# Pre-norm's second half summed by GpSimd, an unscaled first tile, and two tiles closed by halves

## The reference

```python
h = rmsnorm(x, norm_pre[l, n])                    # x * rsqrt(mean(x * x) + eps) * gain
x = x + weight * rmsnorm(sublayer(h), norm_post[l, n])
```

## Time and profile before

| | |
|---|---|
| runs | 2857.49, 2858.16, 2862.65 us, median 2858.16 |
| profiled execution | 2856.87 us, span of its instructions 2854.0 us |
| TensorE's mean granted clock | .991 of full speed |
| VectorE, ScalarE, GpSimd busy | 52%, 37%, 4% of the span |
| products for the sums of x's squares (line 411) | 128, two records each |
| GpSimd's adds (line 1842) | 48 |

### The profile page before, as it was taken

One profiled execution on the slowest core, in us unless ns is written; L12 is line 12 of the kernel. 1 busy time (PEld: TensorE's weight loads), 2 busy tenths in 40 slices (PEclk: granted clock), 3 DMA queues, 4 the chain that ended last, 5 costly groups with the idle time before them and its releaser, 6 DMA issues.

```text
span 2854.0 us, 44258 instructions
## 1 busy us (share of the span) xinstructions
PE 2783.2 (98%) x18986; PEld 2587.9 (91%) x18986; DVE 1487.0 (52%) x2035; ACT 1064.2 (37%) x1559; POOL 106.8 (4%) x124
## 2 busy tenths in 40 slices
PE   8999999998999999999999999999989999999997
PEld 7999999997988889999999999999869988999996
DVE  5555326747564465552365553366576436555423
ACT  4333324325453343332243332242264434333322
POOL 0000000001100100000000000000001001000000
PEclk9999999999999999999999999999999999999998
DMA  4222322222233222232222322222223232222321
GB/s 113 81 81 84 93 82 62 70 73 78 88 105 102 62 67 81 86 88 82 76 74 81 88 86 83 77 73 60 76 78 111 82 95 62 81 86 83 88 84 62
DMA packets 420893, 232.95 MB, mean 82 GB/s; under 512 B 7124, under 2 KB 415736, under 8 KB 420760
## 3 DMA queue, kind: packets, MB, share of 16 engines
q1 hardware_dynamic: 414544, 210.33, 25.5%
q0 software_dynamic: 5984, 20.59, 2.2%
q10 hardware_dynamic: 232, 0.08, 0.0%
HBM read 219.44 MB, written 11.54 MB: 81 GB/s over the span
## 4 chain that ended last, share of the span: by engine, by line
PE 89%; DVE 6%; ACT 3%; DMA 1%; issue 1%; ACTq 0%; POOL 0%; DVEq 0%; POOLq 0%
PE PS L391 36%; PE PS L379 20%; PE PS L393 18%; PE PS L366 4%; PE PS L353 2%; PE PS L830 1%; DVE y_two L1387 1%; PE PS L549 1%; DVE x L1396 1%; PE PS L857 1%; DVE w_lo L1339 1%; DVE h_two L1347 1%; ACT w_hi L929 1%; DMA raw<-in_w_out_dram 1%; PE PS L645 1%
## 5 line engine op out<-in xcount | busy, mean ns | idle before, releaser
L391 PE MATMUL PS<-h_two,w_hi 128*128 128x288 f32 (+2 forms) x4032 | 922.9, 337 | 3.0 <-DVE gt L1418 3.0
L1339 DVE TENSOR_TENSOR w_lo<-raw,w_hi 128x1024 fp32r<-128x1024 f32 (+1 forms) x372 | 490.1, 1317 | 667.1 <-ACT w_hi L929 663.3
L929 ACT ACTIVATE w_hi<-raw 128x1024 fp32r<-128x1024 f32 (+1 forms) x372 | 413.6, 1112 | 592.6 <-DMA raw<-in_ffn_down_dram 268.4
L391 PEld LDWEIGHTS PS<-h_two,w_hi 128*128 128x128 f32 x4032 | 605.5, 188 | 3.7 <-issue 3.7
L393 PE MATMUL PS<-h_two,w_lo 128*128 128x288 f32 x2688 | 571.7, 294 | 0.0
L393 PEld LDWEIGHTS PS<-h_two,w_lo 128*128 128x128 f32 x2688 | 471.8, 188 | 58.3
L391 PE MATMUL PS<-a_two,w_hi 128*128 128x288 f32 (+2 forms) x1848 | 422.8, 337 | 0.0
L379 PE MATMUL PS<-h_two,w_hi 128*128 128x288 f32 x2048 | 381.3, 300 | 2.8 <-DVE proj L1648 1.9
L379 PEld LDWEIGHTS PS<-h_two,w_hi 128*128 128x128 f32 x2048 | 304.7, 189 | 8.1 <-issue 3.6
L391 PEld LDWEIGHTS PS<-a_two,w_hi 128*128 128x128 f32 x1848 | 277.5, 188 | 0.0
L393 PE MATMUL PS<-a_two,w_lo 128*128 128x288 f32 x1232 | 262.0, 294 | 0.0
(11 more groups left out here) (319 smaller groups left out, 3440.9 us busy)
## 6 DMA issues: line engine op xcount, KB each, us to landing
raw<-in_ffn_gu_dram SPq DMA_DIRECT2D x176, 512.0 KB, 3.9
raw<-in_ffn_down_dram SPq DMA_DIRECT2D x64, 704.0 KB, 4.6
raw<-in_w_in_dram SPq DMA_DIRECT2D x52, 512.0 KB, 3.8
raw<-in_w_out_dram SPq DMA_DIRECT2D x16, 512.0 KB, 4.1
raw<-in_w_mk_dram SPq DMA_DIRECT2D x16, 512.0 KB, 3.9
raw<-in_w_mv_dram SPq DMA_DIRECT2D x16, 512.0 KB, 4.0
raw<-in_w_mq_dram SPq DMA_DIRECT2D x16, 512.0 KB, 3.9
raw<-in_w_mo_dram SPq DMA_DIRECT2D x16, 512.0 KB, 4.0
```

The costliest lines, as they stand in the source:

```text
L391: mm(PW[slot][:, j, 0:c1 - c0], wt(ws)(0, k), row[:, c0:c1], start=begin, stop=end and j == 2, skip_group_check=True)
L929: A(whi(c % NW, slice(0, words)), rawu(c % NW, slice(0, words)), ACT.Copy).then_inc(whi_r, 1)
L1339: TT(wlo(c % NW, w_), rawu(c % NW, w_), f32(whi(c % NW, w_)), ALU.subtract).then_inc(wlo_r, 1)
```

## The change

- `pre_piece`, from pn = 1 on and for the second half: the eight squares go to a buffer of eight (`sqh`, two homes in SBUF) instead of the ring of four.
- `add_squares(pn)` on GpSimd, after its adds of the tiles' squares: it waits for the last of the eight squares of norm pn + 1 and adds them up in three instructions (four onto four pieces, two onto two, one onto one).
- TensorE: `opening` has no sums in its second half; one product, `pre_sum_second`, comes ahead of the k-step 1 of the third unit (FFN, IN), or ahead of k-step 4 of the first query unit of MVQ. In MK the sums of the first half stand beside units 1 to 4 and those of the second half are gone.
- The first unit's tile of F1, IN and F2 leaves PSUM by a copy on ScalarE (`raw_tile`), and VectorE scales the copy later.
- MO: `close_two` computes tiles 6 and 7 by halves (6 first half, 7 first half, 6 second half, 7 second half), with the squares, gains and GpSimd's add of tile 6 by halves too.
- The first six of the FFN's wide units are taken out of the loop; the sum of the second post half comes at k-step 1 in every opening.

```diff
@@ GpSimd
             def add_squares(pn):
-                for m in range(1, KD - 1):
-                    pool.wait_ge(psq_r, (KD - 1) * pn + m + 1)
+                whole = KD - 2 if pn % 4 == 2 else KD - 1
+                for m in range(1, whole):
+                    pool.wait_ge(psq_r, squares_before(pn) + m + 1)
...
+                if whole < KD - 1:
+                    pool.wait_ge(acc_r, added_before(pn) + whole - 1)
+                    for h in range(2):
+                        pool.wait_ge(psq_r, squares_before(pn) + whole + 1 + h)
+                        nc.gpsimd.tensor_tensor(acc[:, HALF[h]], acc[:, HALF[h]], sq[:, 0, HALF[h]], ALU.add).then_inc(acc_r, 1)
+                if pn == 4 * DEPTH - 1:
+                    return
+                to = second_home(pn + 1)
+                pool.wait_ge(qsq_r, upto(pn + 1, 1, KD - 1))
+                for n in (4, 2):
+                    nc.gpsimd.tensor_tensor(to[:, 0:n, :], to[:, 0:n, :], to[:, n:2 * n, :], ALU.add).then_inc(pstep, 1)
+                    pool.wait_ge(pstep, 2 * pn + (1 if n == 4 else 2))
+                nc.gpsimd.tensor_tensor(to[:, 0, :], to[:, 0, :], to[:, 1, :], ALU.add).then_inc(qadd_r, 1)
@@ TensorE
+            def pre_sum_second(pn):
+                pe.wait_ge(qadd_r, pn)
+                mm(PX[0][:, 1, 0:HT], ones, second_home(pn)[:, 0, :], start=True, stop=True).then_inc(qsq_d, 1)
+            def close_two(pn, a, t, hi, lo):
+                for h in range(2):
+                    for s in range(2):
+                        u = a + KD - 2 + s
...
+                        for k in range(KD):
+                            m = pieces(u % NW, s, h, k, hi, lo, 0, k == 0, k == KD - 1)
+                            if h == 1 and s == 0 and k == 0:
+                                post_begin(pn, 0)
+                                post_sum(pn, 0)
+                        m.then_inc(unit_d if h else (six_d, half_d)[s], 1)
@@ opening
-                        if h == 0 and k == sum_at:
+                        if h == 0 and k == 1:
+                            if (pn - 1) % 4 == 2:
+                                post_begin(pn - 1, 1)
                             post_sum(pn - 1, 1)
-                        pre_sum(pn, h, k)
+                        if h == 0:
+                            pre_sum(pn, h, k)
@@ ffn (TensorE)
+                for n in range(6):
+                    pe.wait_ge(tile_e, t + 1 + n)
+                    wide_unit(a + 2 + n, n % 2, (a + 2 + n) % NW, h_two, middle={1: lambda: pre_sum_second(pn)} if pn and n == 0 else None)
@@ MK and MVQ (TensorE)
-                    for j in (2 * m, 2 * m + 1):
-                        pre_sum(pn + 1, j // KD, j % KD)
+                    if 1 <= m <= KD // 2:
+                        for k in (2 * m - 2, 2 * m - 1):
+                            pre_sum(pn + 1, 0, k)
...
+                    if m == 0:
+                        beside[4] = lambda: pre_sum_second(pn)
@@ ScalarE
+                if pn and h:
+                    A(second_home(pn)[:, k, :], x[:, k, HALF[h]], ACT.Square).then_inc(qsq_r, 1)
+                    return
...
+            def raw_tile(to, a, slot):
+                act.wait_ge(unit_d, a + 1)
+                A(halves(to), PL[slot][:, :, 0:HT], ACT.Copy).then_inc(tile_e, 1)
...
+                    16: lambda: (raw_tile(proj[:, IN_PLACE[0], :] if pu == "F1" else sg, e, 0), pre_root(pn + 1, 1))})
@@ ffn (VectorE)
-                        v.wait_ge(unit_d, a + 1)
-                        TT(halves(gt[:, :]), PL[0][:, :, 0:HT], halves(rinv[:, :]), ALU.mult).then_inc(tile_e, 1)
+                        v.wait_ge(tile_e, t + 1)
+                        TT(gt[:, :], sg[:, :], rinv[:, :], ALU.mult).then_inc(gt_r, 1)
@@ MO (VectorE)
                 e = a + KD
+                seventh_y(pn, 0)
+                upcoming(e)
                 v.wait_ge(half_d, pn + 1)
                 last_y(pn, 0)
                 post_root(pn, 0)
-                last_y(pn, 1)
-                update(pn, 1.0, {5: lambda: upcoming(e + 1), 7: lambda: post_root(pn, 1)})
+                seventh_y(pn, 1)
+                update(pn, 1.0, {2: lambda: last_y(pn, 1), 5: lambda: upcoming(e + 1), 7: lambda: post_root(pn, 1)})
```

More of the change, by code:

```diff
@@ L109 @@
 WIDE = [(0, HT), (HT, HT + 512), (HT + 512, 2 * T)]
+pairs_before = lambda pn: sum(n % 4 == 2 for n in range(pn))
+squares_before = lambda pn: (KD - 1) * pn + pairs_before(pn)
+added_before = lambda pn: (KD - 2) * pn + pairs_before(pn)
 def hybrid_trunk(nc, i, o):
@@ L166, in hybrid_trunk @@
         mvT = place("mvT", [P, 4, NMEM], F32, G + 23552)
+        sqh = [place(f"sqh{n}", [P, KD, HT], F32, G + w_) for n, w_ in enumerate((19456, 4608))]
         xtok = place("xtok", [P, NCH + 1, D], F32, G)
@@ L382, in unit, with wide_unit @@
                 m.then_inc(unit_d, 1)
-            def wide_unit(u, slot, ws, two, kt=KD, k0=0, first=True, last=True):
+            def wide_unit(u, slot, ws, two, kt=KD, k0=0, first=True, last=True, middle=None):
                 pe.wait_ge(wlo_r, u + 1)
                 for k in range(kt):
+                    if middle and k in middle:
+                        middle[k]()
                     row = two[:, k0 + k, :, :].rearrange("p a t -> p (a t)")
@@ L394, in wide_unit, with post_begin @@
                 m.then_inc(unit_d, 1)
[L396 to L400, removed]
+            def post_begin(pn, h):
+                pe.wait_ge(acc_r, added_before(pn + 1) - (1 if pn % 4 == 2 and h == 0 else 0))
+                mm(PX[1][:, h, 0:HT], ones, acc[:, HALF[h]], start=True, stop=False, skip_group_check=True)
             def post_sum(pn, h):
@@ L469, in ffn @@
                 a, t = unit_base(l, pu), tile_base(l, pu)
-                opening(pn, a, t, sum_at=None if f % 2 else 1)
-                with pe.Fori(0, (2 * KF - 2) // 6) as r:
+                opening(pn, a, t)
+                for n in range(6):
+                    pe.wait_ge(tile_e, t + 1 + n)
+                    wide_unit(a + 2 + n, n % 2, (a + 2 + n) % NW, h_two, middle={1: lambda: pre_sum_second(pn)} if pn and n == 0 else None)
+                with pe.Fori(0, (2 * KF - 2) // 6 - 1) as r:
                     for n in range(6):
-                        pe.wait_ge(tile_e, r * 6 + (t + 1 + n))
-                        wide_unit(r * 6 + (a + 2 + n), n % 2, (a + 2 + n) % NW, h_two)
+                        pe.wait_ge(tile_e, r * 6 + (t + 7 + n))
+                        wide_unit(r * 6 + (a + 8 + n), n % 2, (a + 2 + n) % NW, h_two)
                 b, t = unit_base(l, pd), tile_base(l, pd)
@@ L513, in _ @@
                     pe.wait_ge(tile_e, t + m - 1)
-                    unit(a + m, m % 2, (a + m) % NW, h_hi, h_lo)
+                    unit(a + m, m % 2, (a + m) % NW, h_hi, h_lo, middle={1: lambda: pre_sum_second(pn)} if m == 2 else None)
                 def i_rows():
@@ L894, in _ @@
                 pe.wait_ge(xalo_r, 8 * (l + 1) - 1)
-                for m in range(KD - 1):
+                for m in range(KD - 2):
                     if m >= 2:
@@ L1299, in _ @@
                         side(*jobs[0])
+                    if m == 0:
+                        pre_root(pn, 1)
                     upcoming(a + 2 * m + 3)
```

69 lines of the change are left out of this document (45 added, 24 removed).

## The result

The changed kernel takes 2882.59 us (median of 4 runs, 2879.84 to 2887.90) beside 2858.51 us for the kernel before in the same job (4 runs, 2857.49 to 2862.65): a ratio of 1.0085, with a 95% interval of 1.0073 to 1.0097. The profiled execution took 2879.84 us with a span of 2877.8.

What follows compares the result with a forecast made beforehand. TensorE, busy 98% of the span, was taken as the bound. 2 × 14.1 (load) + 2.45 (pn 4) - 2 × .35 (halves) + 2 × .8 (IN) = +31.55 on 2856.87 us: 2888 us, range 2870 to 2899.

Steps and rivals of the forecast that it cites:

- The load behind the adds: Ahead of MVQ: memory-key load queued behind GpSimd's adds, 12.4 us delay plus 1.7 for the clock, 14.1 a layer.
- S: At each boundary, the moment when the last square of the second half is written.
- The adds' end, P: After the last square: end of GpSimd's last add, put at S + 6.9, lower bound S + 5.3.
- FFN boundary: Second wide unit starts at S + 14.7 instead of S + 12.25, a loss of 2.45 us each.
- IN: At pn 1 and 5: next unit at S + 13.1 instead of S + 12.3, loss .8 us each.
- Halves: At pn 3 and 7: tiles closed by halves bring S 2.8 us earlier, net -.35 us each.
- 23.5 us off TensorE, not on the path: At seven boundaries 49 sums of .48 us go, but the openings' second halves then run at VectorE's pace.
- Rival (b): TensorE's 23.5 us come off whole and the load before MVQ is in time: 2833 us; chance .03.
- Rival (c): TensorE's products come off whole but the load before MVQ stalls: 2858 us, no change; chance .05.
- Rival (a): Same stall before MVQ, but GpSimd never delayed and no fall of the clock: +15.35, 2872 us; chance .17.
- Rival (d): In MK's units without sums the clock falls too, adding 7.8 us to the sum: 2896 us; chance .15.
- The sum: All boundary terms added on the profiled execution of 2856.87 us: +31.55 us, so 2888.4 us.

Runs made afterwards that it cites:

- e1: The changed kernel with the load of the cached memory keys issued ahead of GpSimd's three adds: 2863.14 us, ratio 1.0028.
- e2: The kernel before, with its load of the cached memory keys held back until the last square, all sums on TensorE: 2872.36 us, ratio 1.0056.
- e5: The changed kernel with all of x's squares summed on TensorE and the load in its old place; copy and halves stay: 2846.21 us, ratio .9962.
- e7: e1 with one more GpSimd add of 1152 elements ahead of the three, into an unused spare tile, at all seven boundaries: 2888.67 us, ratio 1.0133.
- e4: The kernel before with only the two tiles of MO closed by halves: 2856.20 us, ratio 1.0001.
- e3: The kernel before with only the unscaled first tile copied on ScalarE, and six units out of the FFN's loop: 2853.80 us, ratio 1.0000.
- e9: e5 with GpSimd's three adds of the squares going into a spare tile that nothing reads: 2852.37 us, ratio .9986.
- e0: e5 without the copy and the halves, leaving the unrolled units and the later second post sum: 2869.26 us, ratio 1.0037.

## Why the prediction was right

The forecast held: slower, 2882.59 us against 2888, inside 2870 to 2899. By its own steps:

- **The load behind the adds.** Predicted 14.1 a layer (12.4 of delay, 1.7 clock); measured 13.7 and 13.5. e1 and e2 show the cause by taking it away and by making it alone. Its parts: the delay was 10.7, counted as predicted from the former start at 817.6 (here 813.8, as MK's last tile came 3.8 us earlier in this trace), since the adds ended at S + 6.3 and not S + 7.3 and the load was in use after 5.2 us and not 5.8; the half clock took 2.2 behind it; and 1.0 was lost in MK, which I had at nothing. Together 13.9. That the sum is so near is in part luck: a delay 1.7 too long stood against .5 of the clock and 1.0 of MK that I had too little.
- **The adds' end, P.** Predicted S + 6.9 (lower bound 5.3); measured S + 6.1 at IN and D2 to F1. VectorE and GpSimd do exclude each other: the split of 1450.36 lasts 2.85 us and ends 1.1 us behind the first add's end (1452.13), the Newton step at 1453.62 lasts 1.19, the second add (1452.21, 576 elements) takes 2.28 us beside that split where such an add takes 1.43, and in MK the third add, .7 us of work, lasts 1.65 as it stands behind a split. The Trainium skill (SBUF — State Buffer, "Who interferes with whom") says that the second to issue is blocked until the first is done, and the trace agrees. What I sized wrong is GpSimd's share: I charged it the whole of a split and a step, 1.6 us, and it lost 1.0; VectorE bears most (1.6 + .7 + .5 us at D2 to F1). The rest of the .8 is the first add, 2.67 us where I had scaled 2.86 from the rows, and smaller hand-overs.
- **FFN boundary.** Predicted +2.45 at pn 4; measured +1.6 (second wide unit at S + 13.9, not 14.7), all of it the smaller P. That a root later than before sets the second wide unit was right: e5, with the old root and the free first tile, starts it earlier (-1.1), e7 with a later one 3.5 us later.
- **IN.** Predicted +.8 each, measured -.1: again P, within the bounds (-.8 to +.8).
- **Halves.** Predicted -.35 net each; measured -1.8 and -1.9. The halves alone give 3.4 (e4) where I had 2.8 for S, and the copy is worth 1.2 more (e3); against them GpSimd's sums cost 2.9.
- **23.5 us off TensorE, not on the path.** Right: its busy time fell by 15.5 us and nothing came of it, the wait for low pieces rose from 5.7 to 12.0 us, MK's units waited 12.7 us for splits, and e5, with all 49 products back, is 16.9 us faster than e1. Rival (b), at 2833, had its place in the load; with the load early (e1) the time was 2863. Rival (c), products off whole and a stalled load, falls with it.
- **Rival (a), 2872:** its two conditions were that GpSimd is never delayed and that the clock does not fall; both are false. **Rival (d), 2896:** its mechanism was there, in small. The clock fell in MK, but for 3.4 us once a layer, and cost 1.0 us each time where (d) had 3.9; in e5 and e9, whose MK units keep their sums, MK's tiles come when they did before.

The sum was 31.55; at the boundaries 24.9 was measured. The difference of 6.6 is 1.0 from MK and MVQ, .85 from D2 to F1, 1.8 from IN and 3.0 from MO to F2. Most of it is one mis-sized term, the adds' end (.8 us too late at D2 to F1, IN and MO to F2, 1.0 in MVQ); .6 us at each MO to F2 is what the halves won beyond my 2.8. The signs are now apart: by the stages the load order costs 22, the sums on GpSimd 16, and the rest of the change wins 13; by the medians it is 18, 17 and 11.

## What to carry to other kernels

Before work is moved to a quiet engine, look at what stands behind it in that engine's queue: a prefetch that was 35 us early became the longest stall of the kernel, and a reordering of two lines took it away. Products taken off a busy TensorE are worth nothing where another engine feeds it piece by piece; there, ask how long the chain from the last piece to the result becomes. And an engine that seems free can still take time from its neighbour: adds that nobody waited for cost 3.1 us at one boundary, half of it by a wait and half behind a fall of the clock.

## What the runs showed of the hardware that I had not expected

- **Two paces of the same FFN stretch.** A k-step of a wide unit takes either .7867 or .7933 us for the whole of an FFN stretch (.85%, some 3 us a stretch), read from the distance of ScalarE's squares over its turns. The profiled execution of the kernel before has .7933 in its first stretch and .7867 in the other three, the kernel after .7867 in all, e0, e4 and e5 .7933 in three. No edit that was made explains it: e5 and e1 run the same loop of wide units, and e1 has .7867 in all four. What sets it stays open. Only profiled executions show it, so how it is spread over the timed runs was not seen, and whether it goes with a kernel neither: e0, e3 and e4 are 4 to 8 us slower by their medians than their boundaries add up to. By an estimate, four stretches of 3 us, it can move a time by up to 12 us, which is why the stages were read beside the medians.
- **Taking turns is not fair in cost.** Three adds of 5.0 us stretched to 6.0 to 6.3, while VectorE's instructions beside them grew by 2.8 (D2 to F1) to 4.1 us (e1, MVQ). That fits an engine losing more where it waits on the longer instruction (an add of 2.7 us against a split of 1.2), but no run varies the lengths.
- **Less work can lower the clock.** A standstill of 11.5 us was followed by half clock for the 5 us of the next unit, one of 7 us (e2) likewise, one of 3.9 us (e7, IN) by 6 us of it, one of 2.1 us by 3.4 us of it in e9 and by none at the same place in e1. In MK merely taking the sums away was enough for 3.4 us of half clock and a loss of 1.0 us, and in e5, with the sums back, it did not fall there. In the openings of IN, where TensorE without sums works .40 us of every 1.17, it fell in the kernel after in both layers (464.4 and 1877.5, 3.4 us each) and in e1 in neither, so what the clock does there also differs between executions.
